# MLP of a one-core transformer kernel: output products over two groups of four token tiles, a reordered start, and block sums of weights on VectorE in place of GpSimd

## The chip, the cores and the metric

The program runs on one core of one Trainium2 chip. The metric is the device time of one execution in microseconds; it is the median over several executions. A core has TensorE (PE, matmuls; its weight loads are PEld), VectorE (DVE), ScalarE (ACT), GpSimd (POOL) and SyncE (SP, which issues most DMAs). Each has its own queue of instructions and works through it in order.

## What is computed

The reference is two transformer blocks over 1024 tokens of width 1024. The change touches the last part, the MLP of the second block and the final norm:

```python
hid = jnp.square(jax.nn.relu(rmsnorm(h, norm_mlp_g[l]) @ w_mlp_in[l]))   # 1024 -> 4096
h = h + hid @ w_mlp_out[l]                                               # 4096 -> 1024
return rmsnorm(h, norm_final_g)
```

## The kernel before

The kernel is written by hand against semaphores. `schedule` (from line 351) writes one list of units; every engine's program walks through that list and takes what concerns it, so the place of a unit in the list is its place on each queue. A `before` hook on SP, ACT, DVE and POOL looks ahead of a unit: SP loads weight panels (512 KB) some panels ahead (`load`, DMA at L3519), ACT makes the rounded high part of a panel (L2778), and DVE (L1837) or POOL (L3280) makes the low part, panel minus high. Every product is then three matmuls of 128x512: high by high, high by low, low by high (`wide`, L1370).

**Start of the MLP.** The products of `w_co` are made in three groups of token tiles (0 to 3, 4 and 5, 6 and 7), and between them each group is normed: ACT squares (L2879), a Newton chain of small DVE instructions (L1948 to L1954), ACT `xhat` (L2888), PE transposes (L1363), ACT copies `feat_x` and `ftm_hi` (L2864, L2865) and DVE `ftm_lo` (L2045), which also frees the bank. `f3` is this step for tiles 6 and 7. The first two chunks of the hidden layer are plain products, `whole(i, l)` for chunk i and token half l, 24 matmuls each. `in_split(0)` halves the first panel into `in_a`, and `in_split_rest(0)`, behind the norm of tiles 6 and 7, halves the second into `in_first` and `in_b`.

**Pairs.** The other 30 chunks are 15 pairs. A pair needs seven products P1 to P7 of a 2x2 block scheme (Strassen-Winograd) in place of eight: 84 matmuls. It takes four block sums of weights (`sums`, POOL, L3476), their high parts `in_s` (ACT, L3215) and low parts `sums_lo` (POOL, L3454), and, once for all pairs, four sums of features (`feature_sums`, DVE L2660 to L2663, high parts ACT L3235, low parts DVE L2666). `in_split(m + 1)` and `in_split_sums(m + 1)` stand ahead of `mlp_pair(m)` in the list. P5 of pair 1 is the first product that needs such sums. DVE adds the products up and squares them (`mlp_pair`), and SP stores them to `hid` in DRAM.

**Output products.** They run over k0, two chunks of 128 hidden rows at a time (16 values), for three groups of token tiles, and each group loads all of `w_mlp_out` again:

```python
GROUPS = ((0, 1, 2, 3), (4, 5), (6, 7))
...
if group == 0 or k0 % 4 == 0:
    chunks = 4 if group else 2
    ph = k.panel("mlp_hid", (group, k0), ...)
```

A k0 of four tiles is 48 matmuls over three panels (one of `hid`, two of weights); a k0 of two tiles is 24 matmuls over two and a half, as its `hid` panel holds four chunks. The panels go round 10 slots (`out_ring`), so a `hid` panel holds its slot for five panels. At the end of a group DVE adds the banks to the residual (L2720), ACT squares, DVE makes the Newton chain, and `final(n)` scales a tile on DVE (L2071) and stores it by SP (L3709), spread over the k0 of the next group. SP's store stands in the same queue as its loads.

Of the kernel before, what the change touches and what calls it, by code (L numbers as in the profile page):

```python
# [350 lines left out]
def schedule(k):  # L351
# [417 lines left out]
    f3, a3 = feats("norm_mlp", (6, 7), (2, 3, 6, 7, 0, 1)), applies("norm_mlp", (6, 7))  # L769
# [20 lines left out]
    def whole(i, l):  # L790
        k.banks.take(("mlp_in", 0, i, l), (((4, 5), (2, 3))[l][i],))
# [12 lines left out]
    k.unit("in_split_sums", 1)  # L804
    outs = []
    for m in range(1, NPAIRS):
# [4 lines left out]
        else:  # L811
            k.out_ring = tuple(k.slot[p] for before in (m - 2, m - 1, m) for p in k.in_panels[before]) + \
                tuple(range(SLOTS, SLOTS + OUT_SLOTS))
            for group, tiles in enumerate(GROUPS):
                for k0 in range(0, NFF2, 2):
                    if group == 0 or k0 % 4 == 0:
                        chunks = 4 if group else 2
                        ph = k.panel("mlp_hid", (group, k0),
                                     rows_of(d["hid"], k0 * P, chunks * P, tiles[0] * P, len(tiles) * P), True)
                        k.hid_key[ph] = min(group, 1), k0 // 2, chunks // 2  # L820
# [5 lines left out]
        for what in PRODUCTS:  # L826
            k.banks.take(("mlp_in", m, what), (4, 5, 6, 7, 0, 1, 2, 3))
# [59 lines left out]
def memory(k, nc, stack):  # L887
# [187 lines left out]
    k.in_first = place("in_first", [P, BANK], F32R, at=at(10))  # L1075
# [13 lines left out]
class Shared(Kernel):  # L1089
# [82 lines left out]
    def in_words(self, m):  # L1172
# [6 lines left out]
        for n in range(4):  # L1179
            words["S%d" % (n + 1)] = self.in_s[s][:, n, :], self.sums_lo[s][n // 2][:, n % 2, :]  # L1180
# [120 lines left out]
def tensor_program(k):  # L1301
# [497 lines left out]
    def mlp_out(h, k0, tiles, pw, ph):  # L1799
        w, x = panel(pw), panel(ph)  # L1800
        for i, n in enumerate(tiles):
            ps = free("mlp_out", h, n) if k0 == 0 else pe.bank("mlp_out", h, n)
            for j in range(2):
                jj = j if len(tiles) == 4 else k0 % 4 + j
                m = wide(ps[:], [y[:, jj, tile(i)] for y in x], [y[:, j, :] for y in w], k0 + j == 0, k0 + j == NFF2 - 1)
            if k0 == NFF2 - 2:
                fill(m, "mlp_out", h, n)
        if k0 != NFF2 - 2:
            m.then_inc(*pe.new("panel_used", pw))

# [5 lines left out]
                c_turn=c_turn, c_weigh=c_weigh, mlp_in=mlp_in, mlp_pair=mlp_pair, mlp_out=mlp_out))  # L1816
# [4 lines left out]
def vector_program(k):  # L1821
# [829 lines left out]
    def feature_sums():  # L2651
        x0, x1 = k.feat_x
        low, high = slice(0, 4), slice(4, KD)
        v.wait_ge("ft_hi", "norm_mlp", 6, KD - 1)

        def did(ins, n):
            ins.then_inc(*v.new("mlp_square", "T", n))
            v.wait_ge("mlp_square", "T", n)

        did(dve.tensor_tensor(x0[:, low, :], x1[:, low, :], x0[:, low, :], ALU.subtract), 1)  # L2660
        did(dve.tensor_tensor(x1[:, low, :], x1[:, high, :], x1[:, low, :], ALU.subtract), 3)
        did(dve.tensor_tensor(x1[:, high, :], x1[:, high, :], x0[:, low, :], ALU.subtract), 2)
        did(dve.tensor_tensor(x0[:, high, :], x0[:, high, :], x1[:, high, :], ALU.subtract), 4)  # L2663
        for n, l, c in ((1, 0, low), (2, 1, high), (3, 1, low), (4, 0, high)):
# [48 lines left out]
    def mlp_out(h, k0, tiles, pw, ph):  # L2713
        if k0 != NFF2 - 2:
            return
        v.wait_ge("resid_loaded", "again")
        for n in tiles:
# [10 lines left out]
               merged=merged, out_turn=out_turn, c_score=c_score, c_finish=c_finish, c_turn=c_turn, c_weigh=c_weigh, mlp_in=mlp_in,  # L2728
               feature_sums=feature_sums, mlp_pair=mlp_pair, mlp_out=mlp_out))
# [4 lines left out]
def scalar_program(k):  # L2734
# [12 lines left out]
    def halve(p):  # L2747
# [3 lines left out]
        elif k.panel_list[p][0] in ("mlp_hid", "mlp_out"):  # L2751
            a.wait_ge(*a.filled("mlp_in", NPAIRS - (2 if k.high_at[p] in [f"True {n}" for n in range(5)] else 1), "P4"))
# [430 lines left out]
    def in_split(m):  # L3183
# [581 lines left out]
```

## Time and profile before

| | us |
|---|---|
| median of 3 executions (2966.23 to 2973.3) | 2972.49 |
| the profiled execution's own time | 2970.01 |
| its span | 2968.8 |
| PE busy in the span | 2821.9 (95%) |
| DVE / ACT / POOL busy | 1658.4 / 1032.1 / 989.5 |

PE is busy nearly always, and 75% of the chain of work that ended last is PE's. So what counts are the few places where PE waits, and the stretches where its granted clock is below full. A busy PE is not PE at its peak: what it could do is read from the distance of two matmuls' starts.

### The profile page before, as it was taken

Reading aid. Unit: us, or ns where it says so; the run is one execution under the profiler, and the core shown is the slowest. Engines: PE = TensorE matmul, PEld = TensorE weight load, DVE = VectorE, ACT = ScalarE, POOL = GpSimd, SP = SyncE. Lnnn points to the kernel's source line nnn. Section 1 sums busy time; section 2 is a strip of 40 time slices with the busy share of each in tenths; the row PEclk is TensorE's granted clock in tenths of the full one; section 3 lists DMA queues with packets and bytes.
Section 4 is the critical chain, followed back from the end, with each engine's and each line's share of the span. In section 5 each row is a group of like instructions: output and inputs, shape, how many; then the busy total and the mean of one; then the engine's idle time right before and its main releaser. Section 6 shows DMA issues by size and latency. Waiting matters only on the chain.

```text
span 2968.8 us, 33195 instructions
## 1 busy us (share of the span) xinstructions
PE 2821.9 (95%) x13188; PEld 2199.7 (74%) x13188; DVE 1658.4 (56%) x2418; ACT 1032.1 (35%) x1577; POOL 989.5 (33%) x565
## 2 busy tenths in 40 slices
PE   6999999999999999999998999999988999999988
PEld 3777567776467888888886678887756888888876
DVE  7556655543874554556556656776345644533454
ACT  2346522223022222222225640674456322132443
POOL 2432012222144444444440214210012877522343
PEclk9999999999999999999999999999998999999999
DMA  7210022214332111111113122113212333364565
GB/s 257 88 41 22 5 82 72 65 57 143 125 94 72 49 50 50 50 49 44 50 43 125 39 57 81 34 42 107 66 42 92 110 110 112 111 227 147 201 235 181
DMA packets 241306, 269.11 MB, mean 91 GB/s; under 512 B 18792, under 2 KB 158464, under 8 KB 241152
## 3 DMA queue, kind: packets, MB, share of 16 engines
q1 hardware_dynamic: 239520, 262.59, 26.9%
q10 hardware_dynamic: 1631, 4.40, 0.4%
q8 instruction: 105, 1.72, 0.2%
q14 instruction: 50, 0.40, 0.0%
HBM read 229.96 MB, written 34.87 MB: 89 GB/s over the span
## 4 chain that ended last, share of the span: by engine, by line
PE 75%; DVE 11%; ACT 6%; DMA 3%; issue 3%; POOL 2%; SPq 0%; ACTq 0%; DVEq 0%; POOLq 0%
PE bank L1370 60%; PE bank L1716 2%; DMA panel<-in_w_mlp_out 2%; PE bank L1518 1%; PE bank L1477 1%; PE bank L1532 1%; PE bank L1700 1%; PE bank L1668 1%; DVE ffn_conv L2403 1%; PE bank L1483 1%; PE bank L1363 1%; DVE ffn_conv L2399 1%; PE bank L1687 1%; DVE mixed L2109 1%; DVE panel_lo L1837 1%
## 5 line engine op out<-in xcount | busy, mean ns | idle before, releaser
L1370 PE MATMUL bank<-ft_hi,panel_lo 128*128 128x512 f32 x1312 | 467.6, 391 | 1.7 <-DVE ftx_lo L2045 1.7
L1370 PEld LDWEIGHTS bank<-ft_hi,panel_lo 128*128 128x128 f32 x1312 | 247.2, 188 | 54.1 <-issue 2.8
L1370 PE MATMUL bank<-ft_hi,panel_hi 128*128 128x512 f32 x704 | 273.9, 389 | 0.0
L1370 PE MATMUL bank<-ft_lo,panel_hi 128*128 128x512 f32 x704 | 273.9, 389 | 0.0
L2399 DVE TENSOR_SCALAR ffn_conv<-ffn_in,ffn_taps 128x512 f32<-128x512 f32 x88 | 114.1, 1297 | 278.8 <-ACT ffn_in L3065 278.6
L3280 POOL TENSOR_TENSOR panel_lo<-panel,panel_hi 128x1024 fp32r<-128x1024 f32 x66 | 158.0, 2401 | 244.3 <-ACT panel_hi L2778 231.1
L1370 PE MATMUL bank<-panelm_hi,panelm_hi 128*128 128x512 f32 x512 | 201.3, 393 | 14.2 <-POOL panel_out_lo L3280 8.6
L1370 PE MATMUL bank<-ft,panel 128*128 128x512 f32 x416 | 202.5, 607 | 2.3 <-ACT sq_inv L3018 0.9
L2403 DVE SCALAR_TENSOR_TENSOR ffn_conv<-ffn_in,ffn_taps,ffn_conv 128x512 f32<-128x512 f32 x176 | 154.5, 878 | 6.2
L1837 DVE TENSOR_TENSOR panel_lo<-panel,panelm_hi 128x1024 fp32r<-128x1024 f32 x52 | 83.5, 1611 | 125.7 <-ACT panelm_hi L2778 125.7
L1370 PEld LDWEIGHTS bank<-ft_hi,panel_hi 128*128 128x128 f32 x704 | 132.1, 188 | 27.5
L1370 PEld LDWEIGHTS bank<-ft_lo,panel_hi 128*128 128x128 f32 x704 | 132.1, 188 | 27.4
L3374 POOL TENSOR_TENSOR ltm_vnew<-lt,masks 128x512 f32<-128x512 f32 x48 | 65.0, 1362 | 249.4 <-PE bank L1518 145.7
L1370 PE MATMUL bank<-panel_hi,ffn_hid_hi 128*128 128x512 f32 x352 | 138.4, 393 | 5.1 <-ACT ffn_in L3065 4.2
L2682 DVE TENSOR_TENSOR mlp_y<-mlp_y,bank 128x512 f32<-128x512 f32 x105 | 72.1, 686 | 125.6 <-ACT mlp_y L3228 74.7
L1370 PE MATMUL bank<-panel_hi,ffn_hid_lo 128*128 128x512 f32 x352 | 138.1, 392 | 0.0
L1370 PE MATMUL bank<-panel_lo,ffn_hid_hi 128*128 128x512 f32 x352 | 138.1, 392 | 0.0
L2778 ACT ACTIVATE panelm_hi<-panel 128x1024 fp32r<-128x1024 f32 x78 | 82.4, 1060 | 148.6 <-DMA panel<-in_w_mlp_out 75.9
L2414 DVE TENSOR_TENSOR resid<-resid,bank 128x512 f32<-128x512 f32 x176 | 111.7, 683 | 35.4 <-PE bank L1370 35.1
L1370 PE MATMUL bank<-panel_lo,panelm_hi 128*128 128x512 f32 x320 | 124.5, 389 | 0.0
L1370 PEld LDWEIGHTS bank<-panelm_hi,panelm_hi 128*128 128x128 f32 x512 | 96.9, 189 | 37.1 <-POOL panel_out_lo L3280 9.4
L2778 ACT ACTIVATE panel_hi<-panel 128x1024 fp32r<-128x1024 f32 x66 | 69.4, 1054 | 140.6 <-PE bank L1370 102.9
(544 smaller groups left out, 6832.4 us busy)
## 6 DMA issues: line engine op xcount, KB each, us to landing
panel<-in_w_mlp_out SPq DMA_DIRECT2D x60, 512.0 KB, 6.7
panel<-in_w_in SPq DMA_DIRECT2D x52, 512.0 KB, 3.8
panel<-in_w_ada SPq DMA_DIRECT2D x48, 512.0 KB, 4.1
panel<-in_ffn_w_up SPq DMA_DIRECT2D x44, 512.0 KB, 3.7
panel_out<-in_w_mlp_out SPq DMA_DIRECT2D x36, 512.0 KB, 6.1
panel<-in_w_mlp_in SPq DMA_DIRECT2D x32, 512.0 KB, 5.1
hid<-mlp_y SPq DMA_DIRECT2D x60, 256.0 KB, 2.0
panel<-in_w_o SPq DMA_DIRECT2D x24, 512.0 KB, 3.5
```

The source lines that it names most:

```text
L1363: m = te.transpose(ps[:, tile(i)], src[:, tile(j)], k.ident[:])
L1370: m = te.matmul(ps, a, b, start=(start and j == 0), stop=(stop and j == len(pairs) - 1))
L1477: m = te.matmul(ps[:, tile(h)], lhs(h), rhs_of(h), start=True, stop=True)
L1716: m = te.matmul(ps[:, at:at + HD + 1], k.p_t[(2 * t + hb) % 4][:, 2 * side + c, :], v, start=(hb == side == c == 0), stop=(hb == side == c ...
L1837: dve.tensor_tensor(lo, k.view(p), hi.bitcast(F32), ALU.subtract).then_inc(*v.new("lowered", p))
L2399: dve.tensor_scalar(out, pre[:, 1 + h * BANK:1 + (h + 1) * BANK], w[:, 0:1], w[:, 3:4], ALU.mult, ALU.add).then_inc(*v.new("ffn_tap", c, g ...
L2403: dve.scalar_tensor_tensor(out, pre[:, 1 + j + h * BANK:1 + j + (h + 1) * BANK], w[:, j:j + 1], out, ALU.mult, ALU.add).then_inc(*v.new("f ...
L2414: evict(dve.tensor_tensor(r, r, v.bank("down", i, h, n)[:], ALU.add), "down", i, h, n)
L2682: return dve.tensor_tensor(out[:], x[:], v.bank("mlp_in", m, what)[:], ALU.add)
L2778: act.activation(k.halves_of(p)[0], k.view(p), ACT.Copy).then_inc(*a.new("halved_hi", p))
L3280: pool.tensor_tensor(lo, k.view(p), hi.bitcast(F32), ALU.subtract).then_inc(*g.new("halved_lo", p))
L3374: pool.tensor_tensor(t.ltm[:], t.lt[:], spread(k.masks[:, lv, :], 1, H4), ALU.mult).then_inc(*g.new("delta_pool", n, "ltm", lv))
```

## The change

1. **Output products** in two groups of four tiles, (0 to 3) and (4 to 7). All `hid` panels hold two chunks. `w_mlp_out` is loaded twice and not three times: 96 panels are handled and not 128. The norm of tiles 0 to 3 is spread over the second group (squares at k0 = 2 to 8, Newton chain at 10, `final` at 12 to 18). The last two k0 of the second group are made by a new unit, `mlp_last`, first for tiles 4 and 5, then for 6 and 7.
2. **Block sums** of weights move from POOL to DVE (a new `in_split` in the vector program); POOL waits for them ahead of its low parts. The buffers of even and odd pairs change places.
3. **Start**: `in_split(0)` halves both panels at once (`in_first` has another place, so it no longer waits for `w_co`); `whole` uses banks 6, 7, 2, 3 in place of 4, 5, 2, 3, and `f3` has banks 0 to 5; the evictions and squares of all four `whole` come in one unit, `squared_whole`, behind the feature sums; `feature_sums` is made in two halves, the first (tiles 4 and 5) ahead of `f3`.

```diff
@@ schedule
-    k.unit("in_split_rest", 0)
+    in_panels(1)
     for i in range(2):
         whole(i, 0)
+    k.unit("feature_sums", 0)
     for step in f3:
         step()
-    in_panels(1)
     k.unit("in_split", 1)
-    k.unit("feature_sums")
+    k.unit("feature_sums", 1)
     for i in range(2):
         whole(i, 1)
+    k.unit("squared_whole")
     k.unit("in_split_sums", 1)
...
-            for group, tiles in enumerate(GROUPS):
+            for group, tiles in enumerate(((0, 1, 2, 3), (4, 5, 6, 7))):
                 for k0 in range(0, NFF2, 2):
-                    if group == 0 or k0 % 4 == 0:
...
+                    ph = k.panel("mlp_hid", (group, k0), rows_of(d["hid"], k0 * P, 2 * P, group * BANK, BANK), True)
...
     between = {(0, 8): [lambda: k.unit("resid_again")],
-               (0, NFF2 - 2): [lambda: norm_start(k, "norm_final", (0, 1, 2, 3))],
...
-               **{(1, 14 + 2 * n): [final(n)] for n in range(4)}, **{(2, 6 + 2 * n): [final(n)] for n in (4, 5)}}
+               (1, 10): [lambda: k.unit("deviation", "norm_final", 0, 4)],
+               **{(1, 2 + 2 * n): [lambda n=n: k.unit("squares", "norm_final", n)] for n in range(4)},
+               **{(1, 12 + 2 * n): [lambda n=n: k.unit("final", n, 0)] for n in range(4)}}
...
+            if group == 0 or k0 < NFF2 - 4:
...
+    for tiles in ((4, 5), (6, 7)):
+        for h in range(HALVES):
+            k.unit("mlp_last", h, tiles, outs[-2:], used=outs[-1][4][1])
+        norm_start(k, "norm_final", tiles)
+        for n in tiles:
+            k.unit("final", n, 0)
@@ vector_program
+    def in_split(m):
...
+        else:
+            v.wait_ge(*v.filled("mlp_in", m - 2, "P4"))
...
+            dve.tensor_tensor(x[n], u, w, op).then_inc(*v.new("lowered", "sum", m, n + 1))
+        v.wait_ge("lowered", "sum", m, 4)
@@ gpsimd_program, in_split
-                pool.tensor_tensor(x[n], u, w, op).then_inc(*g.new("halved_lo", "sum", m, n + 1))
-            g.wait_ge("halved_lo", "sum", m, 4)
+            g.wait_ge("lowered", "sum", m, 4)
@@ tensor_program
+    def mlp_last(h, tiles, outs):
+        for n in tiles:
+            ps = pe.bank("mlp_out", h, n)
+            for _, _, k0, ph, pw in outs:
+                w, x = panel(pw[h]), panel(ph)
+                for j in range(2):
+                    m = wide(ps[:], [y[:, j, tile(n - 4)] for y in x], [y[:, j, :] for y in w], False, k0 + j == NFF2 - 1)
+            fill(m, "mlp_out", h, n)
```

**Order on DVE, from the norm of tiles 6 and 7 to the first feature sums.** Before, the two squares of `whole`, the eight `ftm_lo` of `f3`, then the sums over all columns:

```order
L2670 SCALAR_TENSOR_TENSOR mlp_first_295<-mlp_first_295 128x512 [waits bank4_evicted,deviation_dve]
L2670 SCALAR_TENSOR_TENSOR mlp_first_297<-mlp_first_297 128x512 [waits bank5_evicted]
L2045 SCALAR_TENSOR_TENSOR ftm_lo<-bank,cols,ftm_hi 128x256 [waits ft_hi,bank2_filled]
...
L2045 SCALAR_TENSOR_TENSOR ftm_lo<-bank,cols,ftm_hi 128x256 [waits ft_hi,bank3_filled]
L2660 TENSOR_TENSOR feat_x_274<-feat_x_275,feat_x_274 128x2048
L2661 TENSOR_TENSOR feat_x_275<-feat_x_275 128x2048 [waits mlp_square]
```

Now:

```order
L2672 TENSOR_TENSOR feat_x_274<-feat_x_274,feat_x_275 128x4x256 [waits mlp_square]
L2054 SCALAR_TENSOR_TENSOR ftm_lo<-bank,cols,ftm_hi 128x256 [waits ft_hi,bank0_filled,mlp_square]
...
L2054 SCALAR_TENSOR_TENSOR ftm_lo<-bank,cols,ftm_hi 128x256 [waits ft_hi,bank1_filled]
L2700 TENSOR_TENSOR sums_0_287<-panel_82 128x512 [waits panel_loaded3,panel_loaded2]
L2700 TENSOR_TENSOR sums_0_287<-sums_0_287,panel_81 128x512 [waits lowered]
L2700 TENSOR_TENSOR sums_1_288<-panel_81,panel_82 128x512
L2700 TENSOR_TENSOR sums_1_288<-panel_81,sums_0_287 128x512 [waits lowered]
L2669 TENSOR_TENSOR feat_x_274<-feat_x_275,feat_x_274 128x4x256 [waits lowered]
```

Half of the feature sums now stands ahead of `ftm_lo`; behind it come four weight sums and the other half.

**Order on ACT, from the high parts of the feature sums to the high parts of pair 1's weight sums.** Before:

```order
L3235 ACTIVATE feat_x_hi<-feat_x_275 128x2048
L3235 ACTIVATE feat_x_hi<-feat_x_274 128x2048 [waits mlp_square]
L3220 COPY mlp_first_296<-bank 128x512 [waits bank2_filled]
L3220 COPY mlp_first_298<-bank 128x512 [waits bank3_filled]
L3215 ACTIVATE in_s_286<-sums_0_289 128x1024 [waits halved_lo]
```

Now:

```order
L3277 ACTIVATE feat_x_hi<-feat_x_275 128x2048
L3277 ACTIVATE feat_x_hi<-feat_x_274 128x2048 [waits mlp_square]
L3260 COPY mlp_first_295<-bank 128x512 [waits bank6_filled]
L3260 COPY mlp_first_297<-bank 128x512 [waits bank7_filled]
L3260 COPY mlp_first_296<-bank 128x512 [waits bank2_filled]
L3260 COPY mlp_first_298<-bank 128x512 [waits bank3_filled]
L3253 ACTIVATE in_s_285<-sums_0_287 128x1024 [waits lowered]
```

Two more copies stand ahead of `in_s`.

**Order on SP around the stores of final tiles in the second group** (`panel_79` to `panel_84` and `panel_out` are the ten slots). Before:

```order
L3519 DMA panel_83<-in_w_mlp_out 128x2x512
L3709 DMA out<-resid_227 128x1024 [waits final_scaled]
L3519 DMA panel_84<-hid 128x4x256 [waits moved5,moved3,moved7,moved1,panel_used]
L3519 DMA panel_79<-in_w_mlp_out 128x2x512
L3519 DMA panel_80<-in_w_mlp_out 128x2x512
L3519 DMA panel_out_316<-in_w_mlp_out 128x2x512
L3519 DMA panel_out_317<-in_w_mlp_out 128x2x512
L3709 DMA out<-resid_227 128x1024 [waits final_scaled]
L3709 DMA out<-resid_227 128x1024 [waits out_stored0,final_scaled]
```

Now:

```order
L3544 DMA panel_80<-hid 128x2x512 [waits moved7,moved5]
L3736 DMA out<-resid_227 128x1024 [waits final_scaled]
L3544 DMA panel_out_316<-in_w_mlp_out 128x2x512 [waits panel_used]
L3544 DMA panel_out_317<-in_w_mlp_out 128x2x512
L3544 DMA panel_out_318<-hid 128x2x512 [waits moved3,moved1]
L3736 DMA out<-resid_227 128x1024 [waits final_scaled]
```

A store still stands between loads, with three loads from one to the next, and each three loads now serve 48 matmuls.

## Rows read from the trace of the kernel before

**Rows 1.** The page: span and number of instructions.

```profile
span 2968.8 us, 33195 instructions
```

**Rows 2.** Busy time by stage: start, first sums, pairs, output products.

```profile
core 0: us, PE busy (x) PEld busy (x) DVE busy (x) ACT busy (x) POOL busy (x), PEclk, DMA share, GB/s
2262.80:2309.60 46.80, 36.99 (x136) 28.95 (x136) 28.24 (x30) 25.60 (x39) 20.23 (x10) 0.82 0.12 38
2309.60:2591.70 282.10, 282.06 (x1237) 233.40 (x1238) 149.51 (x170) 61.26 (x73) 210.56 (x114) 0.99 0.34 113
2591.70:2767.70 176.00, 174.39 (x769) 144.07 (x769) 61.36 (x41) 53.67 (x52) 41.52 (x17) 1.00 0.50 181
2767.70:2959.30 191.60, 178.92 (x768) 145.50 (x767) 97.87 (x84) 84.91 (x86) 76.82 (x30) 0.98 0.63 217
```

**Rows 3.** Timeline of PE at the start: start, us, instruction, idle before and releaser.

```profile
2262.85 0.67 PE L1370 MATMUL bank<-ftm_hi,in_a 128*128 128x512 f32 x1 [2.41 <-DVE ftm_lo L2045]
...
2273.85 0.79 PE L1370 MATMUL bank<-ftm_hi,in_first 128*128 128x512 f32 x1 [3.67 <-POOL panel_lo L3454]
...
2274.44 0.63 PE L1370 MATMUL bank<-ftm_lo,in_first 128*128 128x512 f32 x1
2274.87 0.63 PE L1370 MATMUL bank<-ftm_hi,panel_lo 128*128 128x512 f32 x1
...
2288.87 0.80 PE L1370 MATMUL bank<-ftm_hi,in_a 128*128 128x512 f32 x1 [3.20 <-DVE ftm_lo L2045]
...
2309.64 0.47 PE L1370 MATMUL bank<-feat_x_hi,in_s 128*128 128x512 f32 x1 [1.92 <-POOL sums_lo L3454]
```

**Rows 4.** Timeline of ACT, DVE and POOL in the same stretch.

```profile
2267.56 2.19 ACT L2888 ACTIVATE xhat<-resid,rstd 128x1024 f32<-128x1024 f32 x2 [2.41 <-DVE rstd L1954]
2269.66 0.61 ACT L3205 ACTIVATE in_first<-panel 128x512 fp32r<-128x512 f32 x1
...
2289.46 2.28 DVE L2660 TENSOR_TENSOR feat_x<-feat_x,feat_x 128x2048 f32<-128x2048 f32 x1
...
2295.06 4.37 DVE L2662 TENSOR_TENSOR feat_x<-feat_x,feat_x 128x2048 f32<-128x2048 f32 x1
...
2299.47 5.53 ACT L3235 ACTIVATE feat_x_hi<-feat_x 128x2048 fp32r<-128x2048 f32 x3 [5.70 <-DVE feat_x L2662]
2304.90 1.06 ACT L3220 COPY mlp_first<-bank 128x512 f32<-128x512 f32 x2
2305.83 2.03 ACT L3215 ACTIVATE in_s<-sums 128x1024 fp32r<-128x1024 f32 x2
...
2306.99 6.87 POOL L3454 TENSOR_TENSOR sums_lo<-sums,in_s 128x1024 fp32r<-128x1024 f32 x2 [6.40 <-ACT in_s L3215]
```

**Rows 5.** Busy time within one pair of the steady stretch, columns as in rows 2.

```profile
2364.00:2383.00 19.00, 19.00 (x86) 15.73 (x85) 9.11 (x11) 4.13 (x6) 14.21 (x9) 1.00 0.38 124
```

**Rows 6.** Durations ns min/median/max: a POOL block sum, and DVE's low part of a panel.

```profile
L3476 POOL TENSOR_TENSOR sums<-panel,sums x15: 1282/1292/3334, 2289.6 to 2557.9; 128x512 f32<-128x512 f32 x15
...
L1837 DVE TENSOR_TENSOR panel_lo<-panel,panelm_hi x49: 1212/1226/2754, 2603.1 to 2942.0; 128x1024 fp32r<-128x1024 f32 x49
```

**Rows 7.** Waits of PE in groups two and three of the output products: total, times, longest.

```profile
PE bank L1370 <- POOL panel_out_lo L3280: 8.6, 2, 5.0
PE bank L1370 <- POOL panel_lo L3280: 3.5, 3, 2.4
PE bank L1370 <- DVE panel_lo L1837: 0.5, 1, 0.5
```

**Rows 8.** The chain that ended last, in the second group: start, us, what.

```profile
2802.06 6.97 DMA panel<-in_w_mlp_out
...
2812.59 0.36 SPq L3709
...
2814.35 6.67 DMA panel<-in_w_mlp_out
...
2830.73 6.59 DMA panel<-in_w_mlp_out
```

More of the change, by code:

```diff
@@ L813, in schedule @@
                 tuple(range(SLOTS, SLOTS + OUT_SLOTS))
-            for group, tiles in enumerate(GROUPS):
+            for group, tiles in enumerate(((0, 1, 2, 3), (4, 5, 6, 7))):
                 for k0 in range(0, NFF2, 2):
-                    if group == 0 or k0 % 4 == 0:
[L817 to L820, printed above, removed]
+                    ph = k.panel("mlp_hid", (group, k0), rows_of(d["hid"], k0 * P, 2 * P, group * BANK, BANK), True)
+                    k.hid_key[ph] = k0 // 2, group
                     pw = [k.panel("mlp_out", (group, h, k0), rows_of(w_mo, k0 * P, 2 * P, h * BANK, BANK), True)
@@ L2713, in mlp_out, with mlp_last, sums_out @@
     def mlp_out(h, k0, tiles, pw, ph):
-        if k0 != NFF2 - 2:
-            return
+        if k0 == NFF2 - 2:
+            sums_out(h, tiles)
+    def mlp_last(h, tiles, outs):
+        sums_out(h, tiles)
+    def sums_out(h, tiles):
         v.wait_ge("resid_loaded", "again")
@@ L3213, in in_split_sums, with squared_whole @@
         for n in range(2):
-            a.wait_ge("halved_lo", "sum", m, 2 * n + 2)
+            a.wait_ge("lowered", "sum", m, 2 * n + 2)
             act.activation(k.in_s[s][:, 2 * n:2 * n + 2, :], k.sums[s][n][:], ACT.Copy).then_inc(
                 *a.new("halved_hi", "S", m, 12 + 22 * n))
-    def mlp_in(i, l):
-        a.wait_ge(*a.filled("mlp_in", 0, i, l))
-        evict(act.copy(k.mlp_first[2 * i + l][:], a.bank("mlp_in", 0, i, l)[:]), "mlp_in", 0, i, l)
+    def squared_whole():
+        for l in range(2):
+            for i in range(2):
+                a.wait_ge(*a.filled("mlp_in", 0, i, l))
+                evict(act.copy(k.mlp_first[2 * i + l][:], a.bank("mlp_in", 0, i, l)[:]), "mlp_in", 0, i, l)
     def mlp_pair(m):
@@ L3488, in in_split_sums @@
     def in_split_sums(m):
-        s = m % 2
+        s = 1 - m % 2
         for n in range(2):
@@ L3513, in load @@
         if p in k.hid_key:
-            l, first, count = k.hid_key[p]
-            for m in range(first, first + count):
-                for i in range(2):
-                    sp.wait_ge("moved%d" % (4 * (m % 2) + 2 * i + l), "hid", m)
+            m, l = k.hid_key[p]
+            for i in range(2):
+                sp.wait_ge("moved%d" % (4 * (m % 2) + 2 * i + l), "hid", m)
         name = "panel_loaded%d" % k.slot[p]
@@ L3694, in store, with squared_whole @@
         sync.dma_start(d["hid"][tile(2 * m + i), half(l)], y[:]).then_inc(*sp.new("moved%d" % n, "hid", m, step=16))
-    def mlp_in(i, l):
-        sp.wait_ge("mlp_square", 0, i, l)
-        store(0, i, l, k.mlp_first[2 * i + l])
+    def squared_whole():
+        for l in range(2):
+            for i in range(2):
+                sp.wait_ge("mlp_square", 0, i, l)
+                store(0, i, l, k.mlp_first[2 * i + l])
     def mlp_pair(m):
```

126 lines of the change are left out of this document (64 added, 62 removed).

## Prediction

> **What bounds the kernel now.** I read the page first: the span of 2968.8 us [rows 1] is PE's for the most part, so time can only be won where PE waits or runs below its full clock. The busy time by stage says where that is [rows 2]. The pairs (2309.6 to 2591.7) have 282.06 us of PE in 282.10, and the first output group 174.39 in 176.0: nothing to win there, and 174.39/769 gives 0.2268 us for a matmul at full clock. Two stretches are worse. The start of the MLP (2262.8 to 2309.6) has PE busy 36.99 of 46.80 at a granted clock of 0.82. Output groups two and three take 191.6 us for 768 matmuls, which at 0.2268 would be 174.2: an excess of 17.4.
>
> The timeline of PE names the four waits of the start [rows 3]: 2.41 us on `ftm_lo` (bank 4), 3.67 on POOL's low part of `in_first`, 3.20 on `ftm_lo` (bank 2), 1.92 on `sums_lo`. Behind three of them matmuls start 0.43 apart instead of 0.23, as from 2274.44 to 2274.87 [rows 3]: the 1.2 GHz level. Counting rows of that timeline, 8, 15, 11 and 8 matmuls ran so, each costing 0.2 more. The other engines show why the second is so long [rows 4]: `in_first` stands on ACT behind two `xhat` and starts at 2269.66, though its panel had long come.
>
> The waits of PE in the late groups are 8.6 + 3.5 + 0.5 = 12.6 us, all on low parts of panels [rows 7]; the other 4.8 of the 17.4 is slow clock behind them and small idles. The chain that ended last shows their source [rows 8]: a load issued at 2802.06 takes 7 us, then come ACT's high part, DVE's low part and a `final`; its store goes out on SP at 2812.59, and only behind it do the next loads start, 2814.35 and then 2830.73. A round of 12.3 to 16.4 us meets a PE that needs only 24 x 0.2268 = 5.4 us per k0 of two tiles. Weights are loaded as fast as stores let them.
>
> **The output products.** The matmuls stay: 1536 in two groups. Removed are 32 panels of 512 KB (128 to 96) with their high and low parts; no engine that bounds. In the second group a k0 is now 48 matmuls, 10.9 us, with three loads between stores. The low part that the `final` of tile n stands behind belongs to a load that was issued ahead of the store of tile n-1, so the loop has two k0, 21.8 us, for a round of 12.3 to 16.4 [rows 8]: it fits with 5 us to spare at worst. The residual adds and the Newton chain, a block ahead of the 0.5 wait in rows 7, are spread out. A group should then take what the first takes now, 176.0 [rows 2], whose only wait (1.6, at its first weight panel) stays: the panels there come behind the last pair as before. The second has no such start, 174.2 to 176.0. Gain 15.6 to 17.4; I take 16.5. `mlp_last` keeps the tail as it is: the last two tiles' norm, scaling and stores behind the last matmul. Nothing for it.
>
> **The start.** (a) *First wait.* `whole(0, 0)` takes bank 6 and not bank 4, so it need not wait for f2's last `ftm_lo` there; what it needs is the features of tile 5, and `in_first` and `in_b` now stand ahead of ACT's copies for those, up to 0.6 + 0.6 later (0.61 is the `in_first` halving, [rows 4]). Bounds: nothing, or all 2.41 and 8 x 0.2 = 4.0; I take 1.6, as most of the wait is for features anyway. (b) *Second wait.* `in_first` is early, its low part too: 3.67 goes, and 15 x 0.2 = 3.0 with it, 6.7 in all. Cover: the transposes of `f3` come next and need `xhat`, ready about 2270.8 (2267.56 + 2.19 and copies, moved up by what ACT saves); PE gets there about 2272.2. With that cover gone this gain shrinks by what `xhat` is late. (c) *Third wait.* In `f3` bank 2 now holds an earlier chunk of the transposes, so the `ftm_lo` that frees it ends some 2.9 us sooner, and 3.20 shrinks to about 0.3, or is repeated at another place. By (a) and (b) alone `f3` begins 8 to 10 us earlier, and the last `ftm_lo` ends near 2279.3 and not 2289.46, where the first feature sum starts now [rows 4].
>
> (d) *The way to P5 of pair 1*, which decides what (a) to (c) are worth. Today it takes from 2289.5 to 2309.6, 20.1 us [rows 3, 4]. Behind the last `ftm_lo` then stand: on DVE four weight sums (4 x 0.65 = 2.6) and the second half of the feature sums (half of 2.28 is 1.14, half of 4.37 is 2.2: three until ACT may start its last high parts, 3.4 to 6.6, I take 5); on ACT three high parts 5.53, four copies (2 x 1.06 = 2.1; two more than now), the first `in_s` 1.0; on POOL the first `sums_lo`, 6.87/2 = 3.4 [rows 4]. Sum 2.6 + 5.0 + 5.5 + 2.1 + 1.0 + 3.4 = 19.7. So the chain is no shorter, it starts 10.2 sooner and ends 10.6 sooner: P5 at 2299.0. PE would be there near 2292 and stands some 6.5 us, with 15 slow matmuls behind it and not 8: 7 x 0.2 = 1.4 back. **Gain of the start: 10.6 - 1.4 = 9.2**, bounds 5 (feature sums contended in full, `whole` gaining nothing) and 12 (no contention). Two covers are thin. P1 of pair 1 needs POOL's low of `in_a` by about 2286.7, and I expect it at 2284.6 to 2286.5. The sums of pair 2 wait for the `hid` stores of the first chunks, since evictions and squares stand later in `squared_whole`: needed near 2320, expected by 2316.
>
> **The sums on DVE.** 60 of 128x512 leave POOL and come to DVE. The row of a POOL sum has 1.29 us [rows 6], so POOL falls from 14.21 in a pair [rows 5] to about 9.0. On DVE no row shows one. Below: half of a 128x1024 low part, 1.226/2 = 0.61; above: the longest such row, 2.75, met by POOL [rows 6]. I take 0.65, nearest the lower: two reads, same type. DVE has 9.11 of 19.00 busy [rows 5] and comes to 11.8 (9.11 + 2.6), PE stays the bound, and the pairs gain and lose nothing. The way from P4 of one pair, which frees the panels' places, to the last `sums_lo` is 2.6 of sums, 2.0 for `in_s` and POOL's 9.0, 13.6 in all; P5 that needs it comes 84 + 24 matmuls later, 24.5 us: 11 of slack cover it. The Trainium skill (VectorE: DVE Perf Modes, The TRN2 errata) has (N + 151)/0.96 ns for a `tensor_tensor` in fp32, 0.69 us for 512 columns, so the four would be 2.76 and the chain in (d) 0.2 longer.
>
> **The sum.** 16.5 + 9.2 = 25.7 from the profiled execution's own 2970.0: 2944.3, given as **2945**. The profiled one is 2.5 below the median of 2972.5; a median may so stand up to 2.5 higher.
>
> **Rivals.**
> *R1: the start gives nothing.* If one of the thin covers fails (P1 on `in_a`, or sums of pair 2 behind the stores), or the steps in (d) collide, the 10 us that `f3` is earlier turn into a longer wait at P5. For it: the chain in (d) is as long as today's, and gets two copies more. Against: it starts 10 us sooner. Result 2970.0 - 16.5 = 2953.5. Chance 0.17.
> *R2: the store still holds back the loads.* A `hid` slot now looks ahead three panels and not five; if the loop closes over one k0 (10.9) and not two, rounds of 12.3 to 16.4 [rows 8] cost 1.4 to 5.5 at each of four finals, and as much again in the k0 between them, which eats the 16.5. For it: the same store stands between the same loads. Against: by the order, a store waits for the low part of a load that was issued a store earlier. With just the start 2970.0 - 9.2 = 2960.8. Chance 0.09.
> *R3: no change.* R1 and R2 together, 2961 to 2970. Chance 0.06, with other mishaps that end there.
> *R4: slower, DVE becomes the bound of each pair.* DVE and POOL both run longer when they meet: the same 128x2048 sum took 2.28 us alone and 4.37 beside POOL, a POOL sum 1.29 and at most 3.33 [rows 4, 6]. If each sum on DVE took the longest row, 2.75, a pair has 9.11 + 4 x 2.75 = 20.1 of DVE against 19.07 of PE (84 x 0.227). PE then waits 1.05 in each of 14 pairs, and falls to its slow level for some 8 matmuls, 1.6: 14 x 2.65 = 37, less 25.7: 2981. It decides where a sum passes (19.07 - 9.11)/4 = 2.49 us. Against: POOL itself waits for the four sums before its lows of this pair, so they meet little, and it is busy less than half. Chance 0.04.
> By the Trainium skill (SBUF - State Buffer, SBUF: two separate sides) a DVE operation with two SBUF inputs and a GpSimd operation that reads SBUF shut each other out for their whole length. The rows agree as far as they go (4.37 for 2.28); it would make R4 a matter of what POOL runs at the moment a sum is due.
>
> **How the numbers follow.** Forecast as worked out: 0.64. R1 0.17, R2 0.09, R3 0.06, R4 0.04. The own range of the forecast is 15.6 + 5 to 17.4 + 12, so 2940.6 to 2949.4; 2935 allows for waits that go further than I counted, and up to 2960 stand R1 and nearly R2. The kernel's times can tell 0.3%, 8.9 us, from no change. Faster by more: forecast, R1, R2, 0.90. Within: R3, 0.06. Slower: R4, 0.04.
>
> **What would show it.** In the changed profile: no wait at the first `in_first` matmul and a granted clock well above 0.82 until then; one wait of 5 to 8 us ahead of P5 of pair 1 (`feat_x_hi` by `in_s`), at about 2299; sums on DVE at 0.65 to 0.7; a pair still 19.0 us, with DVE near 11.8 and POOL near 9; both output groups 174 to 176 us, with no PE wait on a low part in the second. I am wrong if a wait shows within the pairs, if P5 comes after 2304, or if rounds of load and store in the second group are longer than two k0. R1 shows as P5 near 2309, R2 as waits of PE on low parts in the second group, R4 as PE waiting for DVE each 19 us.

## The result, and the profile after

| | before | changed |
|---|---|---|
| median of 4 executions | 2969.36 us (2965.34 to 2973.3) | 2942.96 us (2941.55 to 2947.93) |
| span of the profiled execution | 2968.8 | 2942.7 |

The ratio is 0.9914, 95% interval 0.9893 to 0.9935: faster by 26.4 us or 0.9%, where 2945 was forecast. The profiled spans differ by 26.1.

The busy time by stage, changed kernel; columns and stages as in [rows 2], whose rows of before these four answer to: from the first plain product to P5 of pair 1, from there to the first output product, and the two output groups.

```profile
2260.00:2299.80 39.80, 29.97 (x139) 24.14 (x137) 35.02 (x43) 27.21 (x44) 9.63 (x4) 0.94 0.18 53
2299.80:2582.80 283.00, 282.94 (x1237) 234.02 (x1238) 170.41 (x226) 61.39 (x73) 128.77 (x58) 0.99 0.34 112
2582.80:2757.70 174.90, 173.22 (x764) 143.12 (x763) 60.38 (x39) 53.07 (x50) 41.66 (x17) 1.00 0.50 183
2757.70:2932.70 175.00, 175.00 (x773) 144.90 (x773) 61.15 (x70) 51.74 (x56) 33.63 (x14) 1.00 0.40 142
```

The second group is 175.0 us of PE in 175.0; groups two and three took 191.6 together [rows 2]. The start has one hole left. The timeline of PE, changed kernel, answers to [rows 3]:

```profile
2249.62 0.66 PE L1364 MATMUL bank<-ident,xhat 128*128 128x128 f32 x4 [2.06 <-DVE ftm_lo L2054]
...
2260.02 0.47 PE L1371 MATMUL bank<-ftm_hi,in_a 128*128 128x512 f32 x1
...
2265.56 0.39 PE L1371 MATMUL bank<-ftm_hi,in_first 128*128 128x512 f32 x1
...
2274.36 0.50 PE L1371 MATMUL bank<-ftm_hi,in_a 128*128 128x512 f32 x1 [0.28 <-DVE ftm_lo L2054]
...
2299.86 0.77 PE L1371 MATMUL bank<-feat_x_hi,in_s 128*128 128x512 f32 x1 [8.88 <-POOL sums_lo L3496]
```

Three of the four waits are gone or nearly so (none ahead of the first `in_a`, none ahead of `in_first`, 0.28 us in place of 3.20 ahead of the second `in_a`), and the fourth, ahead of P5 of pair 1, grew from 1.92 to 8.88. What it is made of stands in the timelines of DVE, POOL and ACT, changed kernel, the counterpart of [rows 4]:

```profile
2277.88 0.68 DVE L2700 TENSOR_TENSOR sums<-panel 128x512 f32<-128x512 f32 x1
...
2280.52 1.22 DVE L2669 TENSOR_TENSOR feat_x<-feat_x,feat_x 128x1024 f32<-128x1024 f32 x1
2281.78 3.32 DVE L2670 TENSOR_TENSOR feat_x<-feat_x 128x1024 f32<-128x1024 f32 x1
2285.13 2.19 DVE L2671 TENSOR_TENSOR feat_x<-feat_x,feat_x 128x1024 f32<-128x1024 f32 x1
...
2280.57 3.44 POOL L3496 TENSOR_TENSOR panel_lo<-panel,in_a 128x1024 fp32r<-128x1024 f32 x1 [27.77 <-DVE sums L2700]
2283.97 2.27 POOL L3496 TENSOR_TENSOR panel_lo<-panel,in_b 128x512 fp32r<-128x512 f32 x1
2295.84 6.65 POOL L3496 TENSOR_TENSOR sums_lo<-sums,in_s 128x1024 fp32r<-128x1024 f32 x2 [9.60 <-ACT in_s L3253]
...
2287.36 5.52 ACT L3277 ACTIVATE feat_x_hi<-feat_x 128x2048 fp32r<-128x2048 f32 x3 [3.58 <-DVE feat_x L2671]
2292.78 2.02 ACT L3260 COPY mlp_first<-bank 128x512 f32<-128x512 f32 x4
2294.68 2.03 ACT L3253 ACTIVATE in_s<-sums 128x1024 fp32r<-128x1024 f32 x2
```

In a pair of the changed kernel (window and columns as in [rows 5]) DVE rises from 9.11 to 11.13 and POOL falls from 14.21 to 8.77, and PE stays full:

```profile
2364.00:2383.00 19.00, 19.00 (x85) 15.73 (x85) 11.13 (x15) 4.18 (x5) 8.77 (x5) 1.00 0.35 111
```

A block sum on DVE (columns as in [rows 6]) lasts 0.69 us:

```profile
L2700 DVE TENSOR_TENSOR sums<-sums,panel x15: 691/692/693, 2278.6 to 2547.0; 128x512 f32<-128x512 f32 x15
```

**A mark to measure from.** The first transposes of the MLP's norm (tiles 0 to 3) stand behind code that the change does not touch. Their rows, of the kernel before, of the changed kernel, and of the changed kernel in a second profile (`changed_again`, below):

```profile
2237.97 0.49 PE L1363 MATMUL bank<-ident,xhat 128*128 128x128 f32 x3
```

```profile
2236.13 0.49 PE L1364 MATMUL bank<-ident,xhat 128*128 128x128 f32 x3
```

```profile
2241.20 0.49 PE L1364 MATMUL bank<-ident,xhat 128*128 128x128 f32 x3
```

So 1.8 of the 26.1 us lie ahead of the change, and the same program moved by 5.1 from one profile to the next. All following profiles are therefore read from this mark. All times are in us; "P5" is the first matmul of P5 of pair 1, and "first output product" the first matmul over `hid`.

| kernel | mark | to P5 of pair 1 | to first output product | first to last output product | mark to end | mark to end, less before |
|---|---|---|---|---|---|---|
| before | 2237.97 | 71.7 | 353.6 | 367.3 | 730.8 | |
| changed | 2236.13 | 63.7 | 346.7 | 349.9 | 706.6 | -24.3 |
| changed_again | 2241.20 | 63.8 | 346.9 | 349.9 | 706.7 | -24.1 |
| out_only | 2234.58 | 70.1 | 353.3 | 350.0 | 713.2 | -17.6 |
| start_only | 2237.13 | 63.0 | 345.5 | 369.9 | 725.3 | -5.6 |
| late_stores | 2237.04 | 70.2 | 351.8 | 352.1 | 713.9 | -17.0 |
| sums_pool | 2240.11 | 61.1 | 343.7 | 349.9 | 703.5 | -27.3 |
| sums_ahead | 2240.31 | 59.0 | 340.9 | 349.9 | 700.7 | -30.1 |
| copies_behind | 2236.14 | 61.5 | 344.0 | 349.9 | 703.9 | -27.0 |
| early_sums | 2240.42 | 57.5 | 337.7 | 350.0 | 697.7 | -33.2 |
| early_sums_held | 2233.84 | 54.7 | 339.1 | 351.7 | 700.7 | -30.2 |
| early_mixed | 2234.56 | 54.7 | 334.8 | 349.8 | 694.6 | -36.2 |

changed_again is the changed kernel once more. 706.6 us from the mark to the end were expected, within 1 us, and 63.7 to P5; it ran 706.7 and 63.8 (median 2942.3 us, ratio 0.9911). The two profiles of the changed kernel agree within 0.3 us in every column behind the mark.

That is not so for every kernel. Before, out_only and late_stores have the same start, and yet reach P5 at 71.7, 70.1 and 70.2. The difference is slow clock: ahead of P5, 31 matmuls of before start 0.43 us apart and not 0.23, the 1.2 GHz level, and 19 in each of the others. Those 12 cost 12 x 0.2 = 2.4 us, less 0.8 by which the wait ahead of P5 is shorter in before. So a difference of 1.5 us or less between two rows of this table says little unless such matmuls are counted.

### The profile page after: what moved, and what is told of

It reads as the page before. It is cut to its first block, busy times and chain, and to the rows that moved or that the text cites. A ratio compares the mean times of both kernels' runs of the same rounds, so it can differ in the third digit from the quotient of the medians.

```text
span 2942.7 us, 33105 instructions
## 1 busy us (share of the span) xinstructions
PE 2809.8 (95%) x13188; PEld 2193.4 (75%) x13188; DVE 1645.6 (56%) x2466; ACT 997.9 (34%) x1545; POOL 856.2 (29%) x489
## 4 chain that ended last, share of the span: by engine, by line
PE 79%; DVE 9%; ACT 6%; issue 2%; POOL 2%; DMA 2%; SPq 0%; ACTq 0%; DVEq 0%; POOLq 0%
PE bank L1371 64%; PE bank L1717 2%; PE bank L1519 1%; PE bank L1478 1%; PE bank L1533 1%; PE bank L1701 1%; PE bank L1669 1%; PE bank L1484 1%; DVE ffn_conv L2412 1%; DVE ffn_conv L2408 1%; PE bank L1364 1%; PE bank L1688 1%; DVE mixed L2118 1%; PE bank L1736 0%; PE bank L1464 0%
## 5 line engine op out<-in xcount | busy, mean ns | idle before, releaser
L1846 DVE TENSOR_TENSOR panel_lo<-panel,panelm_hi 128x1024 fp32r<-128x1024 f32 x40 | 61.6, 1545 | 127.5 <-ACT panelm_hi L2820 127.4
L1371 PE MATMUL bank<-panelm_hi,panel_lo 128*128 128x512 f32 x320 | 124.5, 389 | 0.0
L2820 ACT ACTIVATE panelm_hi<-panel 128x1024 fp32r<-128x1024 f32 x60 | 63.5, 1060 | 171.7 <-PE bank L1371 89.0
```

Source lines behind the costliest of these rows:

```text
L1371: m = te.matmul(ps, a, b, start=(start and j == 0), stop=(stop and j == len(pairs) - 1))
L1846: dve.tensor_tensor(lo, k.view(p), hi.bitcast(F32), ALU.subtract).then_inc(*v.new("lowered", p))
L2820: act.activation(k.halves_of(p)[0], k.view(p), ACT.Copy).then_inc(*a.new("halved_hi", p))
```

## The experiments

**The parts alone: out_only and start_only.**

out_only is the kernel before with

```diff
-            for group, tiles in enumerate(GROUPS):
+            for group, tiles in enumerate(((0, 1, 2, 3), (4, 5, 6, 7))):
```

and the `hid` panels, the norm of the first group and `mlp_last` that belong to it; start_only is the changed kernel with the same lines turned round.

> The kernel before with only the output products in two groups (start, block sums and buffers as before). Theory (the two parts add up): the stretch from the first output product to the last falls by the 17.3 us that the two traces differ by, from 367.3 to about 350, so some 17 us below the kernel before, ratio near 0.994. Rival (the gain of the late stretch hangs on the swapped buffers of the change, which free slots for the first weight panels earlier): 10 us or less, and waits of PE on low parts remain. No wait of PE on a low part in the second group by the first, several by the second.

Measured: ratio 0.995 (0.9937 to 0.9962), 17.6 behind the mark. The output stretch took 350.0 us, with one wait of PE left in it. The waits of PE from the first output product on, of out_only and then of start_only:

```profile
PE bank L1369 <- POOL panel_lo L3292: 1.7, 1, 1.7
```

```profile
PE bank L1372 <- POOL panel_lo L3309: 7.4, 3, 3.9
PE bank L1372 <- POOL panel_out_lo L3309: 6.9, 2, 3.8
PE bank L1372 <- DVE panel_lo L1839: 0.5, 1, 0.5
```

> The changed kernel with the three old output groups: start and block sums alone. Theory: of the 8.75 us by which the first output product comes earlier in the changed kernel, 1.8 stand in the trace already ahead of the start of the MLP, in code that the change does not touch; so 6.9 us below the kernel before, ratio near 0.998, first output product at 352 us or so after the transposes of tiles 0 to 3 (2237.97 and 2236.13 in the two traces) less 6.9. Rival: all 8.75 or the 9.2 of the prediction, ratio 0.997. The 12.6 us of waits on low parts in the late groups are there again.

Measured: ratio 0.9986 (0.9977 to 0.9995), 5.6 behind the mark; the late waits are all there again. The parts add up: 17.6 + 5.6 = 23.2 of 24.3, and the output products carry nearly three quarters. The gain does not hang on the swapped buffers, so the rival of out_only is out.

**What held up the late groups: late_stores.**

In the kernel before SP's store becomes a unit of its own and stands two k0 behind the scaling:

```diff
-    def final(n, n0):
+    def final_store(n, n0):
         sp.wait_ge("final_scaled", n)
...
+            between.setdefault((group, first + 2 * n), []).append(final(n))
+            between.setdefault((group, first + 2 * n + 4), []).append(stored(n))
```

> The kernel before, with only SP's store of each final tile moved two k0 later in the list (four loads or more behind it are then issued without waiting for it). Theory (the late groups' waits come from the loop load, high part, low part, final, store, load): the 12.6 us of waits of PE on low parts in groups two and three fall below 4, and the time is 9 to 14 us below the kernel before, ratio near 0.996. Rival (the panels are late because each slot is freed late or because the DMA queues carry more bytes per matmul in groups of two tiles): waits stay at 8 us or more, time as before within 4 us.

Measured: ratio 0.9953 (0.9941 to 0.9965). The waits of PE on low parts in the whole output stretch, against the 12.6 of [rows 7] and 1.6 at the start of the first group:

```profile
PE bank L1376 <- POOL panel_lo L3286: 1.7, 1, 1.7
PE bank L1376 <- DVE panel_lo L1843: 1.2, 3, 0.5
```

The output stretch fell from 367.3 to 352.1 with three groups, all 128 panels and every byte kept. So 15.2 of the 17.3 us that this stretch wins in the changed kernel were the loop of load, low part, final, store and load that [rows 8] shows, not the number of panels. Two groups give 2.2 more. Moving six stores in the list would have brought most of what the new tiling brought.

**Where the sums stand: sums_pool.**

In the changed kernel DVE's `in_split` goes, and POOL's has again its waits, the four sums and

```diff
-            g.wait_ge("lowered", "sum", m, 4)
...
+                pool.tensor_tensor(x[n], u, w, op).then_inc(*g.new("halved_lo", "sum", m, n + 1))
+            g.wait_ge("halved_lo", "sum", m, 4)
```

> The changed kernel with the block sums back on POOL, all else as changed. Theory (the move to DVE pays nothing in the pairs, and costs 2.6 us at the start, where the four sums stand on DVE between the last ftm_lo and the second half of the feature sums while POOL is idle for 27.8 us): pairs at 19.07 us each as before, P5 of pair 1 some 2 to 2.6 us earlier after f3, time 2 to 2.6 us below the changed kernel. Rival (POOL is needed free): the sums of POOL, 1.29 us each and up to 3.3 beside DVE, make sums_lo late; P5 no earlier or later, or waits within the pairs, time equal or 1 to 5 us above the changed kernel.

Measured: ratio 0.9921 (0.9908 to 0.9935). P5 came 2.7 us earlier and the mark to the end is 3.1 shorter; the wait ahead of P5 is 6.2 in place of 8.9. The pairs have no wait in either. The medians do not show it (2944.9 against 2943.0 and 2942.3 for the changed kernel), since 3 us are less than the 7.4 by which the mark wanders from profile to profile. The trace behind the mark does. So the move of the sums to DVE did nothing for the pairs and cost about 3 us at the start.

**How much room DVE has: sums_x3 and sums_x5.**

In `in_split` of DVE each sum of pairs 2 to 15 is made 2 (or 4) more times:

```diff
+            for again in range(2 if m > 1 else 0):
+                dve.tensor_tensor(x[n], u, w, op).then_inc(*v.new("lowered", "again", m, n, again))
+                v.wait_ge("lowered", "again", m, n, again)
             dve.tensor_tensor(x[n], u, w, op).then_inc(*v.new("lowered", "sum", m, n + 1))
```

> The changed kernel with each block sum of pairs 2 to 15 made three times over on DVE (the same values written again; work added, none left out). Theory (a sum on DVE is free until it takes the slack of a pair, (19.07 - 8.5)/4 = 2.6 us): 3 x 0.7 = 2.1 us for each, DVE 16.9 us of each 19.07, time equal to the changed kernel within 3 us. Rival (what matters is the length of the way from P4 to sums_lo, or the adds queued behind the sums on DVE): waits of PE of 1 us or more in each pair, 15 us or more lost.

> The same with each sum five times. Theory: 3.5 us for each, DVE 8.5 + 14 = 22.5 us per pair against 19.07, so each of 13 or 14 pairs loses 3.4 us and the slow clock behind a wait costs another 1 to 2: 45 to 75 us above the changed kernel. Rival (sums can run in the gaps and DVE is not the bound): under 15 us.

Measured: 2970.4 us, ratio 1.0003 (0.9995 to 1.0012), and 3050.3 us, 1.0271 (1.0258 to 1.0284). Both theories were wrong: threefold sums cost 28 us over the changed kernel and not 3 at most (the rival had said 15 or more), and fivefold sums 108 and not 45 to 75. From P5 of pair 1 to the first output product the changed kernel needs 282.9, these need 299.1 and 381.9. Behind it threefold sums lose 8.5 us more (358.4 for 349.9), most of it in one longer wait, the first low part of an output weight panel:

```profile
PE bank L1371 <- POOL panel_lo L3325: 7.5, 1, 7.5
```

The same wait is 1.7 in the changed kernel, and 12 matmuls at the 0.43 spacing behind it cost 2.3. Why threefold sums already bind within the pairs is in the timelines of DVE and ACT within one pair of sums_x3:

```profile
2413.14 0.69 DVE L2703 TENSOR_TENSOR sums<-panel,sums 128x512 f32<-128x512 f32 x1
2415.63 0.69 DVE L2721 TENSOR_TENSOR mlp_y<-mlp_y,bank 128x512 f32<-128x512 f32 x1 [1.79 <-ACT mlp_y L3271]
...
2413.86 1.06 ACT L3256 ACTIVATE in_s<-sums 128x1024 fp32r<-128x1024 f32 x1 [3.04 <-DVE sums L2703]
2414.83 0.57 ACT L3271 COPY mlp_y<-bank 128x512 f32<-128x512 f32 x1
```

DVE's first add of a pair needs ACT's copy of P1, that copy stands behind `in_s` on ACT, and `in_s` waits for DVE's last sum. In that time, 1.8 us, DVE is idle, in this pair as in a pair of the changed kernel and of sums_x5 (1.79 in all three). The period of a pair is 20.43 us (2395.20 to 2415.63 for the same add); four sums at 3 x 0.69 are 8.3, the idle 1.8, and the rest 10.3, with squares drawn out to 1.7 and 2.4 beside POOL. So 12.1 + 20 x 0.69 = 25.9 for fivefold sums, and the trace of sums_x5 has 26.13 (2402.11 to 2428.24). An estimate from these rows is that a sum may take (19.07 - 12.1)/4 = 1.7 us, and not 2.6, before DVE sets the pace. No run takes the idle away by itself.

**Which work the long wait ahead of P5 is: sums_ahead and copies_behind.**

The changed kernel, first sums_ahead, then copies_behind:

```diff
     k.unit("in_split", 1)
+    k.unit("in_split_sums", 1)
     k.unit("feature_sums", 1)
...
     k.unit("squared_whole")
-    k.unit("in_split_sums", 1)
```

```diff
-    k.unit("squared_whole")
     k.unit("in_split_sums", 1)
+    k.unit("squared_whole")
```

> The changed kernel with the high and low parts of pair 1's block sums ahead of those of the feature sums: on ACT in_s stands before feat_x_hi and the four copies. Theory (the 8.9 us wait ahead of P5 is the queue of ACT: in_s is ready at 2280.5 and starts at 2294.7): sums_lo follows POOL's panel lows and is done by 2293; P5 then waits for the feature sums' low parts only, near 2292 to 2295, a wait of 1 to 4 us in place of 8.9, time 5 to 8 us below the changed kernel, about 2936. Rival (DVE and POOL run longer side by side, 2.19 and 3.32 for sums of 1.22 alone): sums_lo beside the feature sums slows both, P5 at 2297 or later and less than 3 us won.

Measured: ratio 0.9906 (0.9893 to 0.992). The wait is 4.1 and its releaser is now `feat_x_lo` on DVE, P5 4.8 earlier, 5.9 shorter behind the mark: as the theory said (a wait of 1 to 4, 5 to 8 shorter), at its lower end. `sums_lo` then ran beside the feature sums, and DVE's four operations behind the block sums took 10.1 us (2284.7 to 2294.8), where alone they take 4.9.

> The changed kernel with the four copies of the first chunks moved behind pair 1's in_s on ACT. Theory (the way to P5 is ACT's queue): in_s 1.9 us earlier, P5's wait 7.0 in place of 8.9, 1.9 us won from the transposes to the end, 704.7. Rival (the squares and stores of the first chunks, which pair 2's in_s waits for, become late): a new wait ahead of pair 2's P5 and nothing won.

Measured: ratio 0.9919 (0.9905 to 0.9933), wait 6.7, P5 2.2 earlier, 2.7 shorter. The two copies that the change added to this queue, and the two that were there, cost what they last: 2.0 us on ACT. The rest of the 2.7 is mostly slow clock behind a shorter wait (9 matmuls at the 0.43 spacing for 12).

**Taking the sums out of the way: early_sums, early_sums_held, early_mixed.**

early_sums is sums_pool with pair 1's block sums in a unit of their own on POOL, ahead of the plain products:

```diff
     in_panels(1)
+    k.unit("block_sums", 1)
     for i in range(2):
         whole(i, 0)
     k.unit("feature_sums", 0)
+    k.unit("in_split_sums", 1)
...
-    k.unit("in_split_sums", 1)
```

early_sums_held adds a wait in `in_split_sums` of POOL. early_mixed has that wait too, and DVE's `in_split` as in the changed kernel for pairs 2 to 15:

```diff
+        if m == 1:
+            g.wait_ge("mlp_square", "T", 4, 0)
```

```diff
-        if m == 0:
+        if m < 2:
             return
```

> The changed kernel with all block sums back on POOL, and pair 1's sums, their high and low parts moved ahead of the norm features of tiles 6 and 7 (POOL at the sums right behind w_co, ACT in_s behind xhat). Theory (P5 of pair 1 waits only for what stands behind the last ftm_lo: first the queue of ACT, then DVE and POOL running side by side): behind the last ftm_lo only the feature sums remain, POOL has only its two panel lows beside them; P5's wait falls from 8.9 to 0 to 2 us, 7 to 11 us below the changed kernel, 2932 to 2936. Rival 1 (POOL's earlier work slows the first half of the feature sums and the ftm_lo of f3): part of that, 3 to 5 us. Rival 2 (pair 2's block sums, gated by the stores of the first chunks, are late next): a new wait of 3 to 7 us ahead of P5 of pair 2 and little won.

Measured: ratio 0.9891 (0.9878 to 0.9904), 8.9 us shorter than the changed kernel behind the mark, and no wait ahead of P5. Rival 1 took its share: DVE and POOL, early_sums,

```profile
2274.18 1.23 DVE L2672 TENSOR_TENSOR feat_x<-feat_x,feat_x 128x1024 f32<-128x1024 f32 x1
2275.44 3.27 DVE L2673 TENSOR_TENSOR feat_x<-feat_x,feat_x 128x1024 f32<-128x1024 f32 x1
...
2274.95 2.68 POOL L3473 TENSOR_TENSOR sums_lo<-sums,in_s 128x1024 fp32r<-128x1024 f32 x1 [5.98 <-ACT in_s L3230]
```

put `ftm_lo` and the second token half 1.4 us back.

> As early_sums, with POOL's sums_lo of pair 1 held back until the first half of the feature sums is done on DVE. Theory (an operation with two inputs in SBUF on DVE and one on POOL stand still for each other for their whole length: the last sum of the half took 3.27 us in place of 1.22 beside sums_lo, and ftm_lo and PE came 1.4 us later): that sum is back at 1.22, the first matmul of the second token half 38.2 us behind the transposes of tiles 0 to 3 in place of 39.6, P5 at 56.1 in place of 57.5, 696.3 to the end. Rival (sums_lo, then 1.2 us later, pushes POOL's lows of the panels that P1 needs): PE waits for in_a's low ahead of P1 and nothing or less is won.

Measured: ratio 0.9893 (0.9878 to 0.9908). The sum is back at 1.22 and P5 at 54.7, better than the 56.1 expected, yet the end came 3.0 us later than in early_sums. Something else than the rival written down came true. DVE, ACT and PE, early_sums_held:

```profile
2283.66 13.18 DVE L2677 TENSOR_TENSOR feat_x_lo<-feat_x,feat_x_hi 128x2048 fp32r<-128x2048 f32 x4
...
2305.02 2.00 ACT L3230 ACTIVATE in_s<-sums 128x1024 fp32r<-128x1024 f32 x2 [13.70 <-DMA hid<-mlp_first]
2306.93 0.56 ACT L3245 COPY mlp_y<-bank 128x512 f32<-128x512 f32 x1
...
2307.55 0.79 PE L1372 MATMUL bank<-ftm_hi,in_a 128*128 128x512 f32 x1 [2.56 <-ACT mlp_y L3245]
```

POOL's sums of pair 2 ran beside DVE's four low parts, 13.2 us in place of 8.9; squares and stores of the first chunks came late, `in_s` of pair 2 waited for the stores, and the copy of P1 stood behind it. That and the slow clock behind it make 4.2 us from P5 to the first output product (284.4 for 280.2). Another 1.6 lie in the output stretch, where 8 matmuls ran at the 0.43 spacing behind its first wait and none did in early_sums.

> As early_sums_held, but only pair 1's block sums on POOL (early), those of pairs 2 to 15 on DVE as in the change. Theory (in early_sums_held POOL's sums of pair 2 ran beside DVE's low parts of the feature sums, 13.2 us for four in place of 8.9, so the squares and stores of the first chunks came late, in_s of pair 2 waited for them, and the copy of P1 behind it on ACT held a bank, 2.6 us of PE): with the sums on DVE the four low parts take 8.9 again, no wait of 2.6, P5 of pair 1 at 54.7 as there, and 694 to 697 us from the first transposes to the end against 706.6 of the changed kernel and 697.7 of early_sums, so 10 to 12 us below the changed kernel. Rival (the stores are late for another reason, their own DMA time or the queue of SP): the 2.6 us stay and the time is that of early_sums_held.

Measured: 2930.9 us (2923.6 to 2937.5), ratio to the kernel before 0.9874 (0.9857 to 0.9892). The row that decides, DVE of early_mixed:

```profile
2284.40 8.90 DVE L2677 TENSOR_TENSOR feat_x_lo<-feat_x,feat_x_hi 128x2048 fp32r<-128x2048 f32 x4
2293.21 2.49 DVE L2702 SCALAR_TENSOR_TENSOR mlp_first<-mlp_first 128x512 f32<-128x512 f32 x4
```

There is no wait of 2.6, and 694.6 from the mark to the end: 12 us under the changed kernel and the best of all. Against early_sums_held the move of the sums of pairs 2 to 15 to DVE does pay, 4.2 us between P5 and the first output product (280.2 for 284.4), because it keeps POOL still while DVE makes the low parts.

## Why the prediction was right, and where it was not

**The sum.** Forecast -25.7, spans -26.1, of which 1.8 lies ahead of the change. Behind the mark it is -24.3: the output products gave 17.3 where 16.5 was forecast, the start 6.9 where 9.2 was, the tail nothing as forecast. Part of the closeness is luck: the start was forecast 2.3 too high, and the untouched code made up 1.8 of it.

**Output products: right, mechanism and size.** 17.3 is near the upper end of the 15.6 to 17.4 given, and the loop over store and loads was the cause (late_stores). The margin of two k0 was no worry: no wait in the second group. R2 is out. What the text had not weighed is that the loop, not the tiling, was nearly the whole of it.

**First to third wait: right.** (a) gave 1.0 and not 1.6: the two halvings ahead of ACT's copies stand in the way, and the transposes' own wait grew to 2.06 (1.19 before). By (a), (b) and (c) together the first matmul of the second token half is 12.7 us earlier from the mark. `xhat` was in time: it ends at 2269.57, and the transposes that need it start at 2271.01 with no wait. The last `ftm_lo` ended 9.7 us earlier, where 10.2 was said. The slow matmuls were counted a little high: the timeline of before has 8, 13, 10 and 7 starts 0.43 apart and not 8, 15, 11 and 8, which is 0.4 us of term (b), and they stand behind all four waits, not three.

**The way to P5: the term that was mis-sized.** "Sum 2.6 + 5.0 + 5.5 + 2.1 + 1.0 + 3.4 = 19.7" measured, from 2277.88 to 2299.86, 22.0: sums 2.6, feature sums to the third 6.8, high parts 5.5, copies 1.9, `in_s` 1.2, `sums_lo` 4.0. The 5 for the feature sums was taken inside bounds of 3.4 to 6.6 as a middle value; the row lies above the upper one. So P5 came 7.9 and not 10.6 earlier, the wait was 8.88 and not 6.5, and 12 slow matmuls followed where 15 were expected. A middle value was the wrong choice. The DVE operation from 2281.78 to 2285.10 and POOL's from 2280.57 to 2284.01 and from 2283.97 to 2286.24 show why. POOL's first ends 1.09 before DVE's, DVE's 1.14 before POOL's second, POOL's second 1.08 before DVE's next at 2287.32. Alone a DVE operation of this size lasts 1.22, and POOL's second 1.29. By these rows each ran almost only while the other stood. The Trainium skill (SBUF — State Buffer, SBUF: two separate sides) says just that of a DVE operation with two SBUF inputs and a GpSimd one that reads SBUF, and the rows agree. Worked out ahead of time from the durations that the rows of before show, it would have been 3 x 1.22 = 3.7 for the three DVE sums and 2.41 + 1.29 = 3.7 for POOL's two panel lows between them, 7.4 at most and not 5. The rows of before already had it. The 2.28 us that the prediction calls "alone" were not: DVE began at 2289.46 [rows 4], and POOL's sum began just behind it and was the one to be drawn out, 3.33 us for 1.29:

```profile
2289.55 3.33 POOL L3476 TENSOR_TENSOR sums<-panel,sums 128x512 f32<-128x512 f32 x1
```

**R1** did not come: P1 of pair 1 found its low part, pair 2 its stores. But the chain was longer than before, as R1 said, by 1.8 us; and the stores of the first chunks, its second cover, did fail in early_sums_held, where P5 was 9 us earlier and POOL's sums drew out DVE's low parts. In early_mixed, with P5 as early and POOL idle there, it held.

**Block sums on DVE: free in the pairs, right for the price (0.69 us, where 0.65 was taken and 0.69 worked out beside it) and the loads (11.13 for 11.8, 8.77 for 9.0).** "The pairs gain and lose nothing" holds. At the start they cost what they last, about 3 us (sums_pool), which the sum contained as 2.6 without saying that leaving them on POOL would save it.

**R4** is refuted as a forecast, but its point of decision was also wrong: 2.49 us for a sum, worked out from busy time alone. The estimate from sums_x3 and sums_x5 is 1.7, since DVE stands 1.8 us in each pair behind `in_s` and the copy on ACT. Busy shares do not contain an idle that returns every round.

**Not settled.** In start_only the first output product is 8.1 us earlier from the mark, where the changed kernel with the same start is 6.9; 9 matmuls at the 0.43 spacing behind P5 for 12 explain 0.6 of that, the rest is open. Its output stretch is 2.6 longer than before: the waits are 0.6 longer in sum, and 25 matmuls start 0.43 apart for 14, which is 2.2. Medians of 5 cannot tell kernels apart here that lie within 3 us.

## What to carry to other kernels

Where a store and the loads behind it share one queue and the store waits for a computation that waits for a load, the loop closes on itself; look for it in the chain before retiling anything, since moving the store in the list may give most of the gain, as here 15.2 of 17.3 us. When steps are pulled earlier, the gain is capped by the longest queue of work in order behind them: list that queue per engine, and count what both VectorE and GpSimd do with two SBUF inputs there as one queue, not as two. Subtract a mark in untouched code before two profiles are compared for a few us.

## What was not expected of the hardware

The untouched first 2236 us of the program end anywhere from 2233.8 to 2241.2 in fourteen profiles of thirteen kernels, and in two profiles of one kernel 5.1 us apart, while the 706 us behind the mark differ by 0.13 between those two. Squares on DVE (one buffer read twice, 128x512) also met POOL: four of them took 2.5 us with POOL idle (early_mixed) and 6.8 beside `sums_lo` in the changed kernel.
